# Hymba decoder step: decay rows spread by DMA through device memory, keys and y turned by DMA, loads reordered

## The reference

```python
a = rmsnorm(h, norm_mix)
z = a @ w_in                       # u | vg | q | k | vm | o | zi | zf
u = gelu(u); vg = layernorm(gelu(vg))
y_gm = u * (W_s @ vg + b_s)        # per head and chunk of 128 tokens, W_s causal
ig = zi + b_i; lf = log_sigmoid(zf + b_f)
# mLSTM, per head and chunk of L tokens, carry C, n, m:
b = cumsum(lf); g = b + m
D = b[t] - b[s] + ig[s]            # causal, else -inf
m_t = maximum(g, max(D, over s))
s = (q @ k.T) * exp(D - m_t)
num = s @ v + exp(g - m_t) * (q @ C)
den = sum(s) + exp(g - m_t) * (q @ n)
hm = num / maximum(abs(den), exp(-m_t))
C = exp(g[-1] - m_new) * C + (k * w_end).T @ v
y_ml = sigmoid(o) * rmsnorm(hm)    # per head
h = h + concat(y_gm, y_ml) @ w_out
h = h + square(relu(rmsnorm(h, norm_ffn) @ w_up)) @ w_down
h = h + sigmoid(rmsnorm(h, norm_ple) @ w_ple_gate) * (p @ w_ple_proj)
y = rmsnorm(h, norm_final)
```

## Time and profile before

| | us |
|---|---|
| median of 3 runs | 892.16 (890.17 to 940.5) |
| the profiled execution, its own time | 891.83 |
| its span on the slowest core (6) | 890.3 |
| spans of the eight cores | 880.0 to 890.3 |
| PE busy | 856.0 (96% of the span), 5650 matmuls |
| DVE busy | 539.9 (61%) |
| ACT busy | 398.4 (45%) |
| POOL busy | 203.5 (23%) |
| share of PE in the chain that ended last | 86% |
| bytes moved by DMA | 80.57 MB, 91 GB/s |

### The profile page before, as it was taken

How to read it: one execution, slowest core, us unless ns; L and a number is a source line. 1 busy time by engine, 2 the same in 40 slices (tenths; PEclk the granted TensorE clock), 3 DMA queues, 4 the chain that set the end, 5 groups by cost and what they waited for, 6 DMA issues and landing times.

```text
span 890.3 us, 16667 instructions; the slowest of 8 cores (880.0 to 890.3 us)
## 1 busy us (share of the span) xinstructions
PE 856.0 (96%) x5650; PEld 513.1 (58%) x5650; DVE 539.9 (61%) x1080; ACT 398.4 (45%) x776; POOL 203.5 (23%) x312
## 2 busy tenths in 40 slices
PE   3989999999999999889999999999999999999995
PEld 2658666877677755445655555655556545455452
DVE  5858787486876884454544445755544544665566
ACT  2866567766675654351221121211122244645454
POOL 4334224425443242110010000211000011312211
PEclk9999999999999999989999999999999999999999
DMA  8995234125123079851192011682102523432322
GB/s 195 205 182 98 96 119 108 49 49 119 25 49 61 8 116 261 136 103 66 48 142 49 1 48 48 103 181 78 35 24 35 107 50 77 125 89 81 89 69 95
DMA packets 66821, 80.57 MB, mean 91 GB/s; under 512 B 43132, under 2 KB 45440, under 8 KB 65458
## 3 DMA queue, kind: packets, MB, share of 16 engines
q0 software_dynamic: 13648, 32.71, 21.9%
q1 hardware_dynamic: 53090, 46.80, 18.8%
HBM read 81.23 MB, written 18.12 MB: 112 GB/s over the span
## 4 chain that ended last, share of the span: by engine, by line
PE 86%; DMA 6%; ACT 2%; issue 2%; SPq 1%; DVE 1%; POOL 1%; POOLq 0%; ACTq 0%; DVEq 0%
PE pb L252 86%; DMA AR<-AR 3%; ACT AR L252 2%; DMA AR<-w_down 1%; SPq L276 1%; DVE AR L252 1%; DMA AR<-w_u 1%; DMA AR<-xp 1%; POOL SMALL L252 1%; ACT L252 0%; POOLq L283 0%; DVE SMALL L252 0%; ACTq L235 0%; DVEq L235 0%; SPq L235 0%
## 5 line engine op out<-in xcount | busy, mean ns | idle before, releaser
L252 PE MATMUL pb<-AR 128*128 128x512 bf16 (+6 forms) x5280 | 842.2, 320 | 10.2 <-DVE AR L252 6.5
L252 PEld LDWEIGHTS pb<-AR 128*128 128x128 bf16 (+2 forms) x5280 | 488.9, 99 | 343.9 <-issue 24.5
L252 ACT ACTIVATE AR<-pb 128x384 f32<-128x384 f32 (+4 forms) x356 | 171.8, 494 | 372.5 <-PE pb L252 306.5
L252 DVE TENSOR_TENSOR AR<-AR,pb 128x512 f32<-128x512 f32 (+3 forms) x226 | 132.6, 591 | 122.6 <-PE pb L252 122.0
L252 DVE TENSOR_TENSOR AR<-AR 128x384 bf16<-128x384 f32 (+7 forms) x257 | 136.0, 533 | 109.4 <-ACT AR L252 100.7
L252 ACT ACTIVATE AR<-AR 128x1024 bf16<-128x1024 f32 (+7 forms) x178 | 114.2, 674 | 65.4 <-DVE AR L252 35.3
L252 POOL TENSOR_TENSOR SMALL<-SMALL,NEGH 128x1 f32<-128x1 f32 (+1 forms) x102 | 70.1, 691 | 43.2 <-DVE SMALL L252 33.2
L252 POOL TENSOR_SCALAR SMALL<-SMALL 128x1 f32<-128x1 f32 x84 | 25.3, 301 | 236.8 <-ACT AR L252 206.7
L252 ACT ACTIVATE AR<-AR,SMALL 128x1024 bf16<-128x1024 f32 (+1 forms) x61 | 63.1, 1043 | 28.9 <-POOL SMALL L252 20.2
L252 DVE TENSOR_TENSOR AR<-pb,AR 128x258 f32<-128x258 f32 (+3 forms) x86 | 47.6, 580 | 17.2 <-PE pb L252 14.3
L252 POOL TENSOR_TENSOR AR<-AR 128x512 bf16<-128x512 f32 (+2 forms) x37 | 44.6, 1210 | 53.8 <-ACT AR L252 48.7
(11 more groups left out here) (72 smaller groups left out, 198.5 us busy)
## 6 DMA issues: line engine op xcount, KB each, us to landing
AR<-w_up POOLq DMA_DIRECT2D x8, 1024.0 KB, 11.1
AR<-w_down POOLq DMA_DIRECT2D x8, 1024.0 KB, 11.4
y_p<-AR SPq DMA_DIRECT2D x15, 512.0 KB, 2.6
hscr<-AR SPq DMA_DIRECT2D x8, 512.0 KB, 3.9
AR<-xp SPq DMA_DIRECT2D x4, 1024.0 KB, 5.2
AR<-hscr SPq DMA_DIRECT2D x8, 512.0 KB, 6.9
AR<-sC SPq DMA_DIRECT2D x8, 512.0 KB, 4.9
o_Cs<-AR SPq DMA_DIRECT2D x8, 512.0 KB, 3.5
```

Source lines behind the costliest of these rows:

```text
L252: ins = getattr(e, name)(**kw)
```

## The change

G no longer makes the three bf16 parts of the row: it writes RR to a small tensor in device memory (`rscr`, one for each group), and M reads it back for each tile with the same row going to all 128 partitions (256 KB into `big`); DVE then subtracts it from the mask. For all groups but the first, the key blocks are turned by one DMA transpose per tile into `ktok`, and `yml` by one into the tile's part of `KT`, whose layout is now tile by tile; the DVE operations that read PSUM there read SBUF. The one-hot matrix and its set-up go.

At the start N of group 0 and of group 1 are both planned ahead of U of group 0; the u weights wait for a memset in place of the first half tile of x; all other weights wait for group 1's norm (`late`), in another order, with x of group 2 behind w_v. q1 waits for the last operation ahead of the second half of quarter 0 (the norms are done by then) in place of the last hscr read. All of `MOVES` is replaced; two of its 22 lines stand for it.

```diff
 MOVES = """
-B0 -569  B1/pe 15.2  B1 55.2  B2/pe 70.2  B2 52.7  B3/pe 31.8  B3 36.9  C/pe 13.2  C/dve 106.1  G0 -74.9
+B0 -386.7  B1/pe 87  B1 248  B2/pe 239.1  B2 252.2  B3/pe 17.4  B3/act -34.1  B3 33.9  C/pe 3.9  C/act -58.1
...
+    rscr = [nc.dram_tensor(f"rscr{i}", [4, 256], F32, kind="Internal").ap() for i in range(9)]
...
-        SGT, QT, KT = [[A.bf(4 * 256, h4) for _ in range(2)] for _ in range(3)]
+        SGT, QT = [[A.bf(4 * 256, h4) for _ in range(2)] for _ in range(2)]
+        KT = [A.bf(4 * 256, ("p (j h t) -> p h j t", dict(j=2, h=4))) for _ in range(2)]
...
-        OH = A.bf(512, h4)
...
-                if grp is GROUPS[0]:
-                    r[0].rate = 650e3
+                for q in r:
+                    q.rate = 300e3 if q is r[0] and grp is GROUPS[0] else 230e3
...
-        for hp in range(2):
-            dma(WU2[hp].rearrange("p k n -> p (k n)"), w_u2[hp], eng="pool", after=x0[:1])
...
-        for b_ in (ROWX + R3 + DCB):
-            memset("dve", b_, 0.0)
+        for b_ in (ROWX + DCB):
+            q = memset("dve", b_, 0.0)
+            if b_ is ROWX[1]:
+                for hp in range(2):
+                    dma(WU2[hp].rearrange("p k n -> p (k n)"), w_u2[hp], eng="pool", after=[q])
...
-            feat("k", at, n, lambda p, hs: act(KT[d2][:, hs, 0:n], p, AF.Copy, scale=QK_SCALE))
+            feat("k", at, n, lambda p, hs: act(KT[d2][:, hs, 0:n // 128, :], p.rearrange("p h (j t) -> p h j t", t=128),
+                                               AF.Copy, scale=QK_SCALE))
...
-            r3 = R3[d2]
-            act(r3[0:4, 0:n], RR, AF.Copy, scale=-1.0)
-            rl_ = ROWL[32:36, 0:n]
-            stt("dve", rl_, RR, -1.0, r3[0:4, 0:n], ALU.mult, ALU.subtract)
-            cp("dve", r3[32:36, 0:n], rl_)
-            tt("dve", r3[64:68, 0:n], rl_, r3[32:36, 0:n], ALU.subtract)
+            dma(rscr[gi][:, 0:n], RR)
...
-                va, kt, qt = vaug(t), KT[d2], QT[d2]
+                va, kt, qt = vaug(t), KT[d2][:, :, j, :], QT[d2]
                 ktok = KTOK[n % 2] if ty == 0 else KTOKS[:]
-                pk = psb("M")
-                trs([(pk[:, h * 128:(h + 1) * 128], kt[:, h, tk], IDB[:]) for h in range(4)])
-                tt("dve", ktok, pk[:, 0:512].rearrange("p (h d) -> p h d", h=4),
-                   wend.unsqueeze(2).to_broadcast([128, 4, 128]), ALU.mult)
-                pc = ps("M").rearrange("p (h t) -> p h t", h=4)
-                mmx([(pc[:, h, :], OH[:, h, :], r3[:, tk], True, True) for h in range(4)])
-                tt("dve", big, pc, MSK[:, ty, :].unsqueeze(1).to_broadcast([128, 4, 128]), ALU.add)
+                if gi:
+                    dma(ktok, kt.rearrange("p h t -> p (h t)"), transpose=True)
+                    ksrc = ktok
+                else:
+                    pk = psb("M")
+                    trs([(pk[:, h * 128:(h + 1) * 128], kt[:, h, :], IDB[:]) for h in range(4)])
+                    ksrc = pk[:, 0:512].rearrange("p (h d) -> p h d", h=4)
+                tt("dve", ktok, ksrc, wend.unsqueeze(2).to_broadcast([128, 4, 128]), ALU.mult)
+                dma(big, rscr[gi][:, tk].partition_broadcast(128))
+                tt("dve", big, MSK[:, ty, :].unsqueeze(1).to_broadcast([128, 4, 128]), big, ALU.subtract)
...
-                py = psb("M")
-                trs([(py[:, h * 128:(h + 1) * 128], yml[:, h, :], IDB[:]) for h in range(4)])
-                yt = yml
-                stt("dve", yt, SGT[d2][:, :, tk], 1.0, py[:, 0:512].rearrange("p (h t) -> p h t", h=4),
-                    ALU.add, ALU.mult)
+                if gi:
+                    ysrc = yt = kt
+                    dma(yt, yml.rearrange("p h d -> p (h d)"), transpose=True)
+                else:
+                    py = psb("M")
+                    trs([(py[:, h * 128:(h + 1) * 128], yml[:, h, :], IDB[:]) for h in range(4)])
+                    ysrc, yt = py[:, 0:512].rearrange("p (h t) -> p h t", h=4), yml
+                stt("dve", yt, SGT[d2][:, :, tk], 1.0, ysrc, ALU.add, ALU.mult)
...
-            P.tag = f"N{gi}"
-            nops[gi] = stage_N(gi)
+            for g_ in (0, 1) if gi == 0 else (gi,) if gi > 1 else ():
+                P.tag = f"N{g_}"
+                nops[g_] = stage_N(g_)
             if gi == 0:
                 P.tag = "start"
-                load_x(GROUPS[2], nops[0][1:], "pool", one=True)
-                P.tag = "V0"
-                late = [P.ops[-3]]
-                load_win("v", after=late)
+                late = nops[1][1:]
                 dma(CPK[:, 192:512], cpk[:, 192:512], eng="pool", after=late)
                 ws_load(0, BIG[0], "pool", late)
                 dma(rp, rpk[:, 0:2, :], eng="pool", after=late)
                 dma(GROW, gln[0].partition_broadcast(128), eng="pool", after=late)
+                load_win("v", after=late)
+                load_x(GROUPS[2], late, "pool", one=True)
+                load_win("m", after=late)
+                load_x(GROUPS[3], late, "pool")
+                load_win("oqk", after=late)
...
             if gi == 1:
-                load_x(GROUPS[3], nops[1][:1], "pool")
-                load_win("m", after=nops[1][:1])
-                load_win("oqk", after=nops[1][1:])
+                P.tag = "start"
                 load_wout(nops[1])
...
-        q1 = load_q(1, back_h[-1:])
...
+                if (qd, k) == (0, 3):
+                    P.tag = "BN"
+                    q1 = load_q(1, P.ops[-1:])
```

More of the change, by code:

```diff
@@ new lines @@
+G7/dve 5.5  G7 17  G8/act -5.8  G8 -21.6  M1/dve 22.1  M1 -7.4  M2 -47.9  M3/pe 24.2  M3/dve 24.5  M3 11.3
+M4/pe -39.4  M4 65.3  M5 -215.8  M6/act 8.1  M7/dve 14.8  M7 19.7  M8/act -28.3  M8 -8.2  N2/dve -7.6  N2 10.5
+N3/pe -1.6  N3 -58.6  N6/dve 9  N6 31.9  P0 -100.8  P1/pe -1.2  P1 -7.4  P2/pe 19.2  P2 -21.7  P3/pe 1.8  P3 -18.3
+P4/pe 20.9  P4 17.8  P5/pe 31.9  P5 17  P6/pe 37.3  P6 1.7  P7/pe 1.4  P7 79.5  P8/pe 2.7  P8 51.4  SU/pe -26.9
+SU 353.3  U3 104.2  U5 -21.2  U6/pe -15.9  U6 -8.8  U7/pe -4.6  U7 -3.3  V0 4.4  V1/pe -14.1  V1/dve -9.9  V1 3.1
@@ new lines @@
+#1117 10.8  #1132 1.4  #1133 -5.7  #1182 -8.6  #1190 -10  #1208 11.4  #1209 3.2  #1221 2.4  #1224 1.2  #1229 34.2
+#1247 13.5  #1289 9.9  #1294 19.4  #1299 -32.1  #1301 -16  #1306 -21.1  #1313 -8.5  #1314 -11.2  #1332 13.6
+#1336 15.3  #1356 10  #1386 8.3  #1423 -2.2  #1427 18.7  #1430 15.1  #1432 11  #1443 6.5  #1444 6.8  #1448 -27.1
+#1456 -22.6  #1480 1.4  #1489 10.9  #1491 4.5  #1508 -9.5  #1530 -13.9  #1570 21.1  #1583 -2.6  #1629 116
+#1631 -40.3  #1681 86.3  #1934 36  #1951 20.7  #2409 26.9  #2413 30.6  #2426 4.1  #2435 3  #2443 24  #2491 -8.6
@@ L615 @@
+#2495 24.9  #2525 36.4  #2541 -7.8  #2547 22.9  #2563 25.9  #2604 16.6  #2614 18.3  #2629 65.3  #2643 -31.3
+#2649 61.6  #2665 59.5  #2669 -4.1  #2689 24.6  #2729 20.1  #2762 -15.5  #2771 11.3  #2793 11.6  #2829 -13.6
+#2853 35.7  #2891 -29.7  #2893 -103.8  #2895 -172.4  #2897 -105.8  #2905 48.9  #2991 79.9  #3012 -29.4
 """
@@ L883, in build @@
         ROWR = A.f32(256)
-        R3 = [A.bf(256) for _ in range(2)]
         RSEG = [A.f32(40, p=4) for _ in range(2)]
@@ L1188, in stage_G @@
                 dma(o_Ms, rseg[:, 16:32])
-            return aat, ex, dc, r3
+            return aat, ex, dc
         def pair(p, b):
@@ L1242, in stage_M @@
             ut = UT[gi % NAT]
-            aat, ex, dc, r3 = gs
+            aat, ex, dc = gs
             for j, t in enumerate(grp):
@@ L1260, in stage_M @@
                 psc = ps("M").rearrange("p (h t) -> p h t", h=4)
-                mmx([(psc[:, h, :], kt[:, h, tk], qt[:, h, tk], True, True) for h in range(4)])
+                mmx([(psc[:, h, :], kt[:, h, :], qt[:, h, tk], True, True) for h in range(4)])
                 stb = STB[n % 2]
```

43 lines of the change are left out of this document (11 added, 32 removed).

## The result

The changed kernel takes **906.39 us** (median of 4 runs, 904.66 to 907.79), where the kernel before took 891.37 beside it (4 runs): ratio 1.0167, 95% interval 1.0155 to 1.0179. It is slower, by 15 us and clear of noise (under 2% all the same), where I forecast 876.3. Some executions fall into a slower state of the chip: times here are medians of all runs and ratios go by the others alone, and only for experiment 6's first kernel does that make more than 1 us of difference. The profiled execution has a span of 903.1 us on its slowest core, 5.

What follows compares the result with a forecast made beforehand. TensorE was taken as the bound, busy 856.0 us, 96% of the span. Terms -10.3 + 2 + 0 + 0 - 7.5 = -15.8 took 891.83 to 876.0, on the median 876.3 us; own range 870 to 882, wider range 864 to 889.

Steps and rivals of the forecast that it cites:

- step 3: Decay rows written to device memory and read back for each tile: +2 us, bounds 0 and 8.
- rival B: Row reads under the weights' load stop DVE, 8 us in place of 2, start at +3: 885 us; chance 0.20.
- Step 1: 68 one-hot matmuls and 120 transposes removed from PE, all on the path: -10.3 us, other end 15.3.
- the records' price: Removed PE matmuls priced by busy share, 73 and 86 ns each: 15.3 us; as a rival, 868 us, chance 0.20.
- that by starts: Removed PE matmuls priced from start to start in the queue, 55 ns each for 188: 10.3 us.
- step 6: MLP handover, q1 issued after the last norm: 5.8 us idle and 1.75 us of clock regained, -7.5; ends 0 and -8.5.
- Step 2: Fewer VectorE and ScalarE row operations and copies in the front, where PE does not wait for DVE: nothing.
- Step 4: Keys and y turned by 30 DMA transposes on SP, 3.2 us landing mostly covered: cost 0.
- the loaded price: A DMA transpose under load takes 6 us (45.26/7), the cost should cover fail.
- Rival D: DMA round trips, 47 transfers through SP's in-order queue, set the mLSTM's pace: over 2% slower, up to 916 us; chance 0.05.
- Step 5: Start's loads reordered, w_v landing at 31 to 32 us, 26 more fillers: 0, ends -4 and +5.
- the same 29 us of work by 50 us: At the start, PE was said to have done as much work by 50 us as before, supporting the 0.

Runs made afterwards that it cites:

- experiment 6's first kernel: The kernel before with keys and y of groups 1 to 8 transposed by DMA, its own old table kept: 917.34 us (1.0300).
- Experiments 1 and 2: The changed kernel, order untouched, its row reads in 2 KB pieces (1: 892.81 us), or group 0's in 256 B pieces (2: 915.44 us).
- the control: The kernel before with late q1, no other change, and its table of moves fitted anew: 885.56 us (0.9943).
- the square: Four refitted kernels, all with DMA transposes, late q1, matmul rows for groups 0 and 1; start loads and other rows as before or changed: 879.04 to 883.70 us.
- the lower right of the square: The changed kernel with rows of groups 0 and 1 by matmul, the other row reads in 2 KB pieces, table fitted anew: 879.85 us (0.9876).
- the lower left: The changed kernel with rows of all groups by one-hot matmuls, none through device memory, table fitted anew: 883.70 us (0.9914).

## Why the prediction was wrong

**The step that failed is step 3**, "+2, near the lower end", bounds 0 and 8. It measured 24 us of PE's wait. In time, the pieces of 2 KB alone give back 13.6 us with the order untouched; undoing the step gives 22.7 us, undoing it for groups 0 and 1 alone 26.5 (both with a table's scatter of up to 4, and its fitting, in them). The mechanism was on the list: rival B had the late read stop DVE, then PE, for "the place in DVE's queue", and its sign came (PE idle over 8 us from 50 to 316, here 28.2); but its price was 8 us and its time 885. The order list showed the maximum scan and the product that frees the banks right behind the mask additions. What was wrong is the price. I took a loaded read from gln, 14.8 us for 1,074 KB in its queue, divided it by bytes, and got 3.5 us for each 256 KB. But SP's queue advanced by packets beside the load, and gln comes in pieces of 2 KB, the rows in pieces of 512 B. Experiments 1 and 2 show this with nothing else of weight moved: 256 B, 512 B and 2 KB give 915.4, 906.4 and 892.8. The trace of the kernel before held the right price: from 62 to 68 us SP's queue moved 312 packets beside 319 of POOL's, and xs to gln, 594 packets, took the 16.9 us from 57.2 to 74.1, or 28 ns each. By that estimate 1,024 packets are 29 us; 33.9 were measured. Each waits for one of a load that goes on to about 80 us (253 packets of q0 from 76 to 80, 60 from 78 to 82). That bounds the reads by the end of the load, and the last came 4 us short of it, at 75.5. The upper bound had to be that end, not a small delay doubled. The reason that I gave for the lower end, that rows are ready well before PE has the projections, fell with it: the last of their weights, w_k, landed at 67.6 us (26.01 + 41.6), the first read at 68.2 and the second at 75.5.

**Step 1**, -10.3: PE's work without fillers fell from 853.7 to 837.9 us, 15.8, which is nearer the records' price (15.3) than that by starts; but busy time also holds the clock's share, of which the handover's 1.75 us (step 6) is one. In time, transposes by DMA with a fitted table are 3.6 us under late q1 alone and 6.5 under the control, where 120 x 55 ns = 6.6 was forecast; with a scatter of 3 to 4 us the runs do not tell the two prices apart.

**Step 2**, nothing: DVE's busy time fell from 539.9 to 526.6 us, but no run has this step by itself, so what it is worth is not shown.

**Step 4**, nothing: right in the quiet front, with one exception that my own price foresaw. Under the load of w_up a transpose took 11.4 us and PE waited 2.93:

```profile
266.09 11.39 DMA AR<-AR
277.58 0.70 DVE AR L252
278.42 14.51 PE pb L252 x122
```

I saw the loaded price as the cost of a failure, not that w_up's load lies in the front (issued at 265.56 here, at 257.60 before). And the price was misread: the 45.26 us of seven transposes hold SP's waits for ACT, 37.0 us from 340 to 400; what the load changes is the landing, 9.7 us there. Rival D (SP's queue, 916) had the right side and nearly the time, and the wrong place: group 0's reads, not 47 round trips; the two fastest kernels of the square have 30 transposes by DMA, and one of them 13 reads too. The rule quoted there (the Trainium skill, VectorE: DVE Perf Modes, Rules for kernel authors) speaks for TensorE; by the estimate from its figures (section The three transpose paths) 120 blocks would have cost 110 us if each stood on the path. With an order made for them they did not: 879.04 with them on DMA, 882.63 and 885.56 with them on PE.

**Step 5**, 0, ends -4 and +5: V came at 34.59, where I had 31 to 32, and from 22 to 50 us PE was idle 6.5 us with 23 fillers in it (12 more stand ahead of 22 us). The square gives -3.7 and +4.7, so the 0 and its ends came true, but not by the argument: "the same 29 us of work by 50 us" was 22.3 in the changed kernel (31.5 busy less 9.2 of fillers) and 23.3 in the lower right of the square, against 29.2 before. Where those 6 us come back I have not followed, so the 0 is in part luck. The first sixteen u matmuls did take 1.91 us behind 12 fillers, where they took 3.28; yet PEclk reads 1.00 in both stretches, so that it was the clock is not shown. Dense work from 50 us did not come, for step 3's reason.

**Step 6**, -7.5: -8.0 measured with late q1 alone, by the mechanism named: the transposes land in 3.1 us where they took 9.7, PE's wait is gone, and the clock is 1.00 from 381 to 388 us where it was 0.75. In the changed kernel the transposes issued from 343 to 390 us landed in 11.3 us (median), with eight hscr reads, issued from 349.92, ahead of most of them on SP's queue, and those from 365 to 400 us in 3.7; PE waited for none of them, and its clock is 1.00 there too.

Account: 876.3 + 26.5 (step 3, by the square's lower right) + 3.6 (that kernel less the forecast, within a table's scatter) = 906.4. Both terms are taken from the same run, so that they add up proves nothing; with the lower left they are 22.7 and 7.4.

## What to carry to other kernels

Price a small transfer beside a bulk load by its number of packets and by what one turn took in a trace, and take the end of the bulk load as its upper bound; the quiet landing time holds only where the other queue is empty. Moving a row through device memory belongs where no load runs, and in pieces as long as the layout allows; then ask what stands behind it in its own DMA queue and behind its reader. And an edit to a kernel whose order is fixed by a fitted table must be judged with the table fitted again, against a control that was fitted in the same way and with as many shifts: the same edit gave 917 and, with late q1, 879 here, and the fitting itself scattered by 3 to 4 us. A planner that is told of a late transfer must be told what the queue behind it does as well.

The fastest of the fourteen kernels are the kernel before with late q1 and transposes by DMA, 879.04, and the lower right of the square, 879.85, which the runs do not tell apart; late q1 alone, three lines, gives 882.63.
